# Down products of the six mixers: token block 0 of the first weight piece ahead of the wait for the last outputs

## The chip, the cores and the metric

The kernel runs on one core of one Trainium2 chip, as one program. The metric is the time of one execution on the device, in microseconds (us); lower is better. The time before is the median of three runs.

## What is computed

Two stacks of layers, one behind the other, work on 256 tokens of 1024 values (`x`), all in float32. The first stack has a layer with forgetting attention and one with latent attention, each followed by a mixture of 16 experts. The second has four layers, each a mixer and a squared-ReLU MLP: retention, MoBA attention, differential attention, retention. Each of the six mixers ends with the same step, a product of its outputs with an output matrix (its "down product"), added to `x`:

```python
return o @ w_o                                        # forgetting attention, latent attention
return ((jax.nn.silu(g) * o) @ w_out).astype(h.dtype) # retention: o is 256 x 2048, w_out 2048 x 1024
return (o @ w_out).astype(h.dtype)                    # MoBA, differential attention: o is 256 x 1024
x = x + m
```

In retention `o` has 4 heads of 512 values; in the attentions it has 16 heads of 64 (8 of 128 in the differential one).

## The kernel before

**Engines and order.** Every engine has its instructions written out in program order; semaphores tie them together. There is no scheduler. TensorE does all products and all transposes ("turns"). Float32 precision comes from splitting each operand into a high part and a low part (the rest): a product is high x high, low x high and high x low, three matmuls where one would do.

**The weights.** SyncE streams them in pieces of 128 x 2048 values into a ring `raw` of three. ScalarE copies a piece to its high part (`w_high`, L1813, two instructions), which it may do once `piece_done` says that TensorE is through with the piece three before it. VectorE subtracts to get the low part (`w_low`, L2271). Both rings have three slots, so up to three pieces are ready ahead of TensorE. TensorE waits for `high_ready` (`wait_high`) and `low_ready` (`wait_low`).

**The tokens.** The 256 tokens are two blocks of 128 (`TB` = 2). The sum of a down product, `y_sum`, is the whole PSUM tensor `Y`: token block 0 in its columns 0 to 1023, block 1 in 1024 to 2047.

**A down product** (`down_product`) takes a chunk of 512 rows of the weights as two pieces. Of a piece it does, for both token blocks, 16 matmuls with the high part of the weights (L1169 with the high part of the input, L1171 with the low part), then waits for the low part and does 8 more (L1179): 24 matmuls of 512 columns. The very last piece of a mixer is done block by block (L1159 to L1161), so that VectorE can start to add block 0 to `x`. Attention has 2 such chunks (4 pieces), retention 4 (8 pieces).

**What stands ahead of it in attention.** Eight rounds of heads. Of the last one TensorE weighs the values (`weigh(7)`, L1310) into `o_ps`, which is `Y`'s columns 1024 to 2047. VectorE then splits the turned first half of the outputs (`o_low(0)`, L2334, in the differential layer L2338; it frees the pair buffer of `a.oT[0]`), and after that takes the last round's output out of PSUM (`finish(7)`: L2431, and L2438 or in the differential layer L2440), which raises `o_taken`. TensorE waits for both before the first matmul of the down product. The second half of the outputs is turned between the first piece and the second (`turn_rest`).

**What stands ahead of it in retention.** Head h is weighed into half h % 2 of `Y` (L1601 to L1603). ScalarE squares it (L1826), POOL makes the root mean square (L927, L929), VectorE scales and gates it into `r_o` (`finish(h)`, L2810 and twice L2816), which raises `r_taken`. TensorE turns head h with `turn_round(h)` (8 transposes, L1191) into the pair buffer of `r.oT[h]`; ScalarE and VectorE copy it out in a high part (L1881) and a low part (L2334). Heads 0 and 1 are turned inside the loop, and then come

```python
turn_round(2)
turn_round(3)
for j in range(4):
    wait_emptied(pe, r.oT[j])
    down_product(r.wo[j], *r_blocks(j), j == 0, j == 3)
```

`turn_round(3)` waits for head 3 (half 1 of `Y`), and the first chunk of the down product behind it needs head 0 alone as its input.

Of the kernel before, what the change touches and what calls it, by code (L numbers as in the profile page):

```python
# [14 lines left out]
P = 128  # L15
S = 256
TB = S // P
# [360 lines left out]
def build(nc, w, table, out, rel_scratch):  # L378
# [3 lines left out]
    with ctx:  # L382
# [176 lines left out]
        y_sum = Y[:, :].rearrange("p (b n) -> p b n", b=TB)  # L559
# [15 lines left out]
        piece_done = sem("piece_done")  # L575
# [64 lines left out]
        o_taken = sem("o_taken")  # L640
# [57 lines left out]
        def r_blocks(j):  # L698

            if j < 2:  # L700
                return hT_high[:, 4 * j:4 * j + 4, :], hT_low[:, 4 * j:4 * j + 4, :]
            return gated_high[:, j - 2], gated_low[:, j - 2]
# [270 lines left out]
        def _(pe):  # L973
# [10 lines left out]
            def wait_low(s):  # L984

                pe.wait_ge(low_ready, s + 1)
# [152 lines left out]

                mod_product(m, first_mods[m]).then_inc(modulated, 1)  # L1140

            def down_product(c, high_in, low_in, first, last_one, between=None):

                for j in range(2):
                    if j and between is not None:
                        between()
                    s = 2 * c + j
                    high, low = high_piece(s, 2, D), low_piece(s, 2, D)
                    wait_high(s)
                    if last_one and j == 1:  # L1150

                        wait_low(s)
                        for b in range(TB):
                            bs = slice(b * P, (b + 1) * P)
                            for n in range(2):
                                y, ns = y_sum[:, b, n * 512:(n + 1) * 512], slice(n * 512, (n + 1) * 512)
                                for k in range(2):
                                    hi_in, lo_in = high_in[:, 2 + k, bs], low_in[:, 2 + k, bs]
                                    nc.tensor.matmul(y, hi_in, high[:, k, ns], start=False, stop=False)  # L1159
                                    nc.tensor.matmul(y, lo_in, high[:, k, ns], start=False, stop=False)  # L1160
                                    last = nc.tensor.matmul(y, hi_in, low[:, k, ns], start=False, stop=(k == 1))  # L1161
                            last.then_inc(piece_done if b else first_block_done, 1)
                        continue
                    for b in range(TB):
                        for n in range(2):
                            y, ns = y_sum[:, b, n * 512:(n + 1) * 512], slice(n * 512, (n + 1) * 512)
                            for k in range(2):
                                kk = 2 * j + k
                                nc.tensor.matmul(y, high_in[:, kk, b * P:(b + 1) * P], high[:, k, ns],  # L1169
                                                 start=(first and kk == 0), stop=False)  # L1170
                                nc.tensor.matmul(y, low_in[:, kk, b * P:(b + 1) * P], high[:, k, ns],  # L1171
                                                 start=False, stop=False)
                    wait_low(s)
                    for b in range(TB):
                        for n in range(2):
                            y, ns = y_sum[:, b, n * 512:(n + 1) * 512], slice(n * 512, (n + 1) * 512)
                            for k in range(2):
                                kk = 2 * j + k
                                last = nc.tensor.matmul(y, high_in[:, kk, b * P:(b + 1) * P], low[:, k, ns],  # L1179
                                                        start=False, stop=False)  # L1180
                    last.then_inc(piece_done, 1)
# [75 lines left out]
            def attention(a, dh, q, k, v, qT, kT, o, dv, o_wait, v_wait, gate_at=None, q_wait=None):  # L1257
# [81 lines left out]
                    o_wait(1)  # L1339
                    transposes(a.oT[1], tokpair(o), 4)  # L1340

                pe.wait_ge(o_taken, a.unit + 8)
                for j in range(2):
                    wait_emptied(pe, a.oT[j])
                    down_product(a.wo[j], hT_high[:, 4 * j:4 * j + 4, :], hT_low[:, 4 * j:4 * j + 4, :], j == 0, j == 1,
                                 None if j else turn_rest)

            def attention_done(a):
                def wait(j):
# [223 lines left out]
            def retention(r):  # L1573
# [32 lines left out]
                def turn_round(h):  # L1606
                    pe.wait_ge(r_taken, r.head + h + 1)
                    transposes(r.oT[h], r_o, 4 * h)
# [6 lines left out]
                        turn_round(h - 2)  # L1615
                    weigh(h)
                turn_round(2)
                turn_round(3)
                for j in range(4):
                    wait_emptied(pe, r.oT[j])  # L1620
                    down_product(r.wo[j], *r_blocks(j), j == 0, j == 3)


            pe.wait_ge(rows_loaded, 16 * early)
# [13 lines left out]
            for j in range(6):  # L1638
# [3 lines left out]
                if j == 0:  # L1642
# [5 lines left out]
                                     start=False, stop=True).then_inc(fill_done, 1)  # L1648
                elif j < 5:
                    wait_free(pe, use)  # L1650
                    ps = quads(pair(use)[:, :])
                    for i in range(4):
# [5 lines left out]
                        last = nc.tensor.matmul(ps[:, i, P:S], f1, upto_m, start=False, stop=True)  # L1658
# [21 lines left out]
            for bank in range(4):  # L1680
                for b in range(TB):
                    if b or bank >= 2:
                        turn_latent(b, bank)
                        last = turn_latent(b, bank + 4)
# [37 lines left out]
            for b in range(TB):  # L1722
                for k in range(2):
                    last = nc.tensor.transpose(quads(pair(use)[:, :])[:, k, b * P:(b + 1) * P],
                                               ckv[:, b, k * P:(k + 1) * P], ident)
# [1371 lines left out]
```

## Time and profile before

| | |
|---|---|
| median of 3 runs | 2613.46 us (2613.22 to 2613.64) |
| the profiled execution | 2617.71 us |
| its span, first to last instruction | 2615.9 us |
| TensorE busy | 2463.7 us, 94% of the span, 12650 matmuls |
| VectorE / ScalarE busy | 1699.8 us (65%) / 1318.9 us (50%) |
| mean granted TensorE clock | 0.974 |
| HBM | 533.54 MB read, 206 GB/s over the span |

A busy TensorE is one with a matmul in its pipeline; what it does in a stretch depends also on the clock that it was granted there, full (1.00, 2.4 GHz) or half (0.50, 1.2 GHz). The profiled execution took 4.25 us more than the median of the runs without a profile.

### The profile page before, as it was taken

The numbers are of one execution on the slowest core, as the hardware profiler recorded it, in microseconds if no ns is written. First come the engines' busy times: TensorE is split into PE (matmuls) and PEld (weight loads), VectorE is DVE, ScalarE is ACT, GpSimd is POOL, SyncE is SP. The second block draws the span as 40 slices with busy tenths as digits, with TensorE's granted clock in tenths as the row PEclk, the third lists the DMA queues.
The fourth block names the chain that finished last, engine by engine and source line by source line (L and its number), as shares of the span: only waits on it lengthen the run. The fifth ranks groups of instructions, "written<-read, shape, count | busy, mean of one in ns | idle before, by whom it ended". The sixth has DMA issues, their size and how long they took to land.

```text
span 2615.9 us, 31350 instructions
## 1 busy us (share of the span) xinstructions
PE 2463.7 (94%) x12650; PEld 2082.9 (80%) x12650; DVE 1699.8 (65%) x1521; ACT 1318.9 (50%) x1795; POOL 93.8 (4%) x121
## 2 busy tenths in 40 slices
PE   4989999999989999899999999899997999999999
PEld 3878777787778778779878887688876888987887
DVE  5767888787868776767445555555566655644555
ACT  3555677443646665643444444544445544443543
POOL 1000000101100000000000001000001000000000
PEclk8998999998998999999999999999999999999999
DMA  8714999984716887964535584245551555553553
GB/s 288 276 46 166 319 348 331 364 314 140 285 38 233 312 310 270 337 212 141 195 114 182 177 271 167 91 161 193 193 176 51 185 193 193 177 194 113 177 193 129
DMA packets 229568, 539.80 MB, mean 206 GB/s; under 512 B 20880, under 2 KB 27568, under 8 KB 229424
## 3 DMA queue, kind: packets, MB, share of 16 engines
q1 hardware_dynamic: 207264, 471.82, 51.4%
q0 software_dynamic: 15520, 59.77, 6.4%
q10 hardware_dynamic: 6640, 6.20, 1.2%
q8 instruction: 100, 1.64, 0.2%
q14 instruction: 44, 0.36, 0.0%
HBM read 533.54 MB, written 4.19 MB: 206 GB/s over the span
## 4 chain that ended last, share of the span: by engine, by line
PE 66%; DVE 15%; DMA 8%; ACT 6%; issue 3%; POOL 1%; SPq 1%; ACTq 0%; DVEq 0%; POOLq 0%
PE pair L1032 7%; DVE w_low L2271 6%; PE Y L1169 6%; PE Y L1171 6%; PE Y L1179 6%; PE pair L1073 4%; PE pair L1067 4%; PE pair L1068 4%; PE pair L1040 4%; DMA raw<-in_exp_w_gate 3%; ACT w_high L1813 3%; DMA raw<-in_exp_w_down 3%; PE pair L1002 2%; PE pair L1004 2%; PE pair L1010 2%
## 5 line engine op out<-in xcount | busy, mean ns | idle before, releaser
L2271 DVE TENSOR_TENSOR w_low<-raw,w_high 128x2048 fp32r<-128x2048 f32 (+2 forms) x450 | 1020.7, 2275 | 568.0 <-ACT w_high L1813 565.4
L1813 ACT ACTIVATE w_high<-raw 128x1024 fp32r<-128x1024 f32 (+1 forms) x900 | 910.1, 1050 | 729.9 <-PE Y L1179 202.4
L1067 PE MATMUL pair<-w_high,hT 128*128 128x512 f32 (+1 forms) x596 | 232.4, 391 | 1.3 <-ACT work L1868 0.8
L1068 PE MATMUL pair<-w_high,hT 128*128 128x512 f32 (+1 forms) x596 | 231.0, 388 | 0.0
L1169 PE MATMUL Y<-w_high,gated_high 128*128 128x512 f32 x528 | 205.8, 390 | 0.0
L1171 PE MATMUL Y<-w_high,gated_low 128*128 128x512 f32 x528 | 205.8, 390 | 0.0
L1032 PE MATMUL pair<-hT,w_high 128*128 128x512 f32 x768 | 183.0, 390 | 2.3 <-DVE work L2717 2.3
L1032 PEld LDWEIGHTS pair<-hT,w_high 128*128 128x128 f32 x768 | 142.5, 188 | 31.6 <-DVE work L2717 2.7
L1475 PE MATMUL Y<-w_high,gated_high 128*128 128x512 f32 x320 | 131.4, 411 | 28.0 <-DVE gated_low L2615 23.3
L1431 PE MATMUL pair<-w_high,rounded 128*128 128x512 f32 x384 | 154.1, 401 | 2.7 <-DVE gated_low L2615 2.7
L1432 PE MATMUL pair<-w_high,rounded 128*128 128x512 f32 x384 | 151.6, 395 | 0.0
L1073 PE MATMUL pair<-w_low,hT 128*128 128x512 f32 (+1 forms) x596 | 146.6, 388 | 4.5 <-DVE w_low L2271 4.5
L1073 PEld LDWEIGHTS pair<-w_low,hT 128*128 128x128 f32 x596 | 110.7, 188 | 28.9 <-DVE w_low L2271 6.6
L1067 PEld LDWEIGHTS pair<-w_high,hT 128*128 128x128 f32 x596 | 112.7, 189 | 25.1 <-issue 1.5
L1068 PEld LDWEIGHTS pair<-w_high,hT 128*128 128x128 f32 x596 | 112.7, 189 | 22.4
L1179 PE MATMUL Y<-w_low,gated_high 128*128 128x512 f32 x528 | 130.4, 389 | 0.0
L1477 PE MATMUL Y<-w_high,gated_low 128*128 128x512 f32 x320 | 128.7, 402 | 0.0
L1002 PE MATMUL pair<-hT,w_high 128*128 128x256 f32 x512 | 126.0, 286 | 0.4
L1004 PE MATMUL pair<-hT,w_high 128*128 128x256 f32 x512 | 125.1, 284 | 0.0
L1179 PEld LDWEIGHTS Y<-w_low,gated_high 128*128 128x128 f32 x528 | 99.1, 188 | 20.6
L1169 PEld LDWEIGHTS Y<-w_high,gated_high 128*128 128x128 f32 x528 | 99.2, 188 | 19.9 <-issue 0.2
L1171 PEld LDWEIGHTS Y<-w_high,gated_low 128*128 128x128 f32 x528 | 99.2, 188 | 19.9
(391 smaller groups left out, 4052.7 us busy)
## 6 DMA issues: line engine op xcount, KB each, us to landing
raw<-in_exp_w_gate SPq DMA_DIRECT2D x128, 512.0 KB, 4.5
raw<-in_exp_w_up SPq DMA_DIRECT2D x128, 512.0 KB, 4.8
raw<-in_exp_w_down SPq DMA_DIRECT2D x128, 512.0 KB, 4.6
raw<-in_w_up SPq DMA_DIRECT2D x128, 512.0 KB, 4.7
raw<-in_w_down SPq DMA_DIRECT2D x128, 512.0 KB, 4.4
raw<-in_ret_w_in SPq DMA_DIRECT2D x96, 512.0 KB, 4.7
work<-in_w_mod POOLq DMA_DIRECT2D x40, 1024.0 KB, 7.8
raw<-in_ret_w_out SPq DMA_DIRECT2D x32, 512.0 KB, 4.1
```

What stands on the lines that cost most here:

```text
L1002: nc.tensor.matmul(ps[:, f, :], high[:, k, f * P:(f + 1) * P], hT_high[:, kk, :], start=(kk == 0 and f % 2 == 0), stop=False)
L1004: nc.tensor.matmul(ps[:, f, :], high[:, k, f * P:(f + 1) * P], hT_low[:, kk, :], start=False, stop=False)
L1032: nc.tensor.matmul(ps[:, f, :], high[:, k, fs], hT[:, :, kk, :], start=(kk == 0), stop=False)
L1067: nc.tensor.matmul(ps[:, b, 0:n], in_high[:, k0 + kk, bs], high[:, k, :], start=(kk == 0), stop=False)
L1068: nc.tensor.matmul(ps[:, b, 0:n], in_low[:, k0 + kk, bs], high[:, k, :], start=False, stop=False)
L1073: last = nc.tensor.matmul(ps[:, b, 0:n], in_high[:, k0 + kk, b * P:(b + 1) * P], low[:, k, :], start=False, stop=(kk == k_blocks - 1))
L1169: nc.tensor.matmul(y, high_in[:, kk, b * P:(b + 1) * P], high[:, k, ns], start=(first and kk == 0), stop=False)
L1171: nc.tensor.matmul(y, low_in[:, kk, b * P:(b + 1) * P], high[:, k, ns], start=False, stop=False)
L1179: last = nc.tensor.matmul(y, high_in[:, kk, b * P:(b + 1) * P], low[:, k, ns], start=False, stop=False)
L1431: nc.tensor.matmul(out(m, v), x_high, high[:, k, :], start=(h == 0 and k == 0), stop=False)
L1813: nc.scalar.activation(w_high[:, s % HIGH, part], raw[:, s % RAW, part], ACT.Copy).then_inc(high_ready, 1)
L2271: V.tensor_tensor(w_low[:, s % HIGH, 0:n], part, w_high[:, s % HIGH, 0:n].bitcast(F32), ALU.subtract).then_inc(low_ready, 1)
```

## The change

For the first piece of each mixer's down product, `down_product` gets a function `second_block`. Then the piece is done token block by token block: 8 matmuls with the high weights and 4 with the low ones for block 0, then the call of `second_block`, then the same 12 for block 1. In attention `second_block` is the wait for `o_taken`, which stood ahead of the whole product; in retention it is `turn_round(3)`, with its wait for `r_taken`. Nothing else is changed, on no other engine.

```diff
+                    if j == 0 and second_block is not None:
+
+                        for b in range(TB):
+                            bs = slice(b * P, (b + 1) * P)
+                            if b:
+                                second_block()
+                            for part in (high_in, low_in):
+                                for n in range(2):
+                                    y, ns = y_sum[:, b, n * 512:(n + 1) * 512], slice(n * 512, (n + 1) * 512)
+                                    for k in range(2):
+                                        nc.tensor.matmul(y, part[:, k, bs], high[:, k, ns],
+                                                         start=(first and part is high_in and k == 0), stop=False)
+                            if b == 0:
+                                wait_low(s)
+                            for n in range(2):
+                                y, ns = y_sum[:, b, n * 512:(n + 1) * 512], slice(n * 512, (n + 1) * 512)
+                                for k in range(2):
+                                    last = nc.tensor.matmul(y, high_in[:, k, bs], low[:, k, ns], start=False, stop=False)
+                        last.then_inc(piece_done, 1)
                         continue
...
-                pe.wait_ge(o_taken, a.unit + 8)
+                def outputs_taken():
+                    pe.wait_ge(o_taken, a.unit + 8)
+
...
-                                 None if j else turn_rest)
+                                 None if j else turn_rest, None if j else outputs_taken)
...
-                turn_round(3)
+
+                def turn_last():
+                    turn_round(3)
+
                 for j in range(4):
                     wait_emptied(pe, r.oT[j])
-                    down_product(r.wo[j], *r_blocks(j), j == 0, j == 3)
+                    down_product(r.wo[j], *r_blocks(j), j == 0, j == 3, second_block=None if j else turn_last)
```

TensorE's order in the first retention, from the last matmul of head 3 on; before, with both turns ahead of the product:

```order
L1603 MATMUL Y<-work 128x512
L1191 MATMUL pair<-squares,work 128x128 [waits emptied1,r_taken]
L1191 MATMUL pair<-squares,work 128x128 x7
L1191 MATMUL pair<-squares,work 128x128 [waits emptied0,r_taken]
L1191 MATMUL pair<-squares,work 128x128 x7
L1169 MATMUL Y<-w_high,hT 128x512 [waits high_ready,emptied1]
L1171 MATMUL Y<-w_high,hT 128x512
...
L1179 MATMUL Y<-w_low,hT 128x512 [waits low_ready]
L1179 MATMUL Y<-w_low,hT 128x512 x7
```

The same place in the changed kernel (the turns are L1211 there, the matmuls of the first piece L1174 and L1181):

```order
L1625 MATMUL Y<-work 128x512
L1211 MATMUL pair<-squares,work 128x128 [waits emptied1,r_taken]
L1211 MATMUL pair<-squares,work 128x128 x7
L1174 MATMUL Y<-w_high,hT 128x512 [waits high_ready,emptied1]
L1174 MATMUL Y<-w_high,hT 128x512 x7
L1181 MATMUL Y<-w_low,hT 128x512 [waits low_ready]
L1181 MATMUL Y<-w_low,hT 128x512 x3
L1211 MATMUL pair<-squares,work 128x128 [waits emptied0,r_taken]
L1211 MATMUL pair<-squares,work 128x128 x7
L1174 MATMUL Y<-w_high,hT 128x512 x8
L1181 MATMUL Y<-w_low,hT 128x512 x4
```

Twelve of the 24 matmuls of the first piece now stand between the turn of head 2 and the turn of head 3.

TensorE's order in the differential attention, from the last weighing on; before:

```order
L1310 MATMUL Y<-work 128x128 [waits o_taken,pT_ready]
L1310 MATMUL Y<-work 128x128 x7
L1169 MATMUL Y<-w_high,hT 128x512 [waits high_ready,emptied0,o_taken]
L1171 MATMUL Y<-w_high,hT 128x512
...
L1179 MATMUL Y<-w_low,hT 128x512 [waits low_ready]
L1179 MATMUL Y<-w_low,hT 128x512 x7
L1191 MATMUL pair<-squares,work 128x128 [waits emptied1,o_ready]
```

And in the changed kernel:

```order
L1330 MATMUL Y<-work 128x128 [waits o_taken,pT_ready]
L1330 MATMUL Y<-work 128x128 x7
L1174 MATMUL Y<-w_high,hT 128x512 [waits high_ready,emptied0]
L1174 MATMUL Y<-w_high,hT 128x512 x7
L1181 MATMUL Y<-w_low,hT 128x512 [waits low_ready]
L1181 MATMUL Y<-w_low,hT 128x512 x3
L1174 MATMUL Y<-w_high,hT 128x512 [waits o_taken]
L1174 MATMUL Y<-w_high,hT 128x512 x7
L1181 MATMUL Y<-w_low,hT 128x512 x4
L1211 MATMUL pair<-squares,work 128x128 [waits emptied1,o_ready]
```

The wait for `o_taken` has moved behind the first 12 matmuls; the wait for the freed pair buffer (`emptied`) stays ahead of them.

## Rows read from the trace of the kernel before

**Rows 1.** The page, part 1: span, and busy time of each engine.
```profile
span 2615.9 us, 31350 instructions
PE 2463.7 (94%) x12650; PEld 2082.9 (80%) x12650; DVE 1699.8 (65%) x1521; ACT 1318.9 (50%) x1795; POOL 93.8 (4%) x121
```

**Rows 2.** Waits of PE: waiter <- releaser: us in total, times, longest us.
```profile
PE Y L1310 <- ACT work L1934: 26.4, 28, 2.7
...
PE pair L1191 <- DVE work L2816: 6.3, 4, 2.8
...
PE Y L1169 <- DVE work L2438: 2.2, 3, 0.7
...
PE Y L1169 <- DVE work L2440: 2.1, 1, 2.1
```

**Rows 3.** Timeline of PE, first retention (start, duration, instruction, idle before).
```profile
1349.05 1.09 PE L1191 MATMUL pair<-squares,work 128*128 128x128 f32 x8 [0.38 <-DVE work L2816]
1352.91 1.97 PE L1191 MATMUL pair<-squares,work 128*128 128x128 f32 x8 [2.77 <-DVE work L2816]
1354.53 0.77 PE L1169 MATMUL Y<-w_high,hT 128*128 128x512 f32 x1
1355.11 0.63 PE L1171 MATMUL Y<-w_high,hT 128*128 128x512 f32 x1
...
1358.91 0.39 PE L1169 MATMUL Y<-w_high,hT 128*128 128x512 f32 x1
1359.14 0.40 PE L1171 MATMUL Y<-w_high,hT 128*128 128x512 f32 x1
...
1362.11 0.39 PE L1169 MATMUL Y<-w_high,hT 128*128 128x512 f32 x1
```

**Rows 4.** Timeline of DVE and of ACT, first retention.
```profile
1334.29 2.28 DVE L2271 TENSOR_TENSOR w_low<-raw,w_high 128x2048 fp32r<-128x2048 f32 x1
...
1348.91 1.22 DVE L2334 TENSOR_TENSOR hT<-pair,hT 128x1024 fp32r<-128x1024 f32 x1
...
1351.45 1.41 DVE L2816 SCALAR_TENSOR_TENSOR work<-Y,head_rs,work 128x512 f32<-128x512 f32 x2
...
1355.97 1.23 DVE L2334 TENSOR_TENSOR gated_low<-pair,gated_high 128x1024 fp32r<-128x1024 f32 x1 [1.98 <-ACT gated_high L1881]
1364.35 2.29 DVE L2271 TENSOR_TENSOR w_low<-raw,w_high 128x2048 fp32r<-128x2048 f32 x1 [7.15 <-ACT w_high L1813]
...
1362.31 2.01 ACT L1813 ACTIVATE w_high<-raw 128x1024 fp32r<-128x1024 f32 x2 [6.37 <-PE Y L1179]
```

**Rows 5.** Windows around the first turn 3: engines, then PEclk, DMA share, GB/s.
```profile
1349.05:1352.02 2.97, 1.09 (x8) 0.85 (x8) 1.81 (x3) 2.14 (x5) 0.89 (x2) 1.00 0.00 0
1352.02:1358.85 6.83, 5.94 (x18) 5.06 (x19) 3.19 (x4) 1.02 (x1) 0.00 (x0) 0.50 0.00 0
```

**Rows 6.** Timeline of PE, second retention.
```profile
2384.15 1.97 PE L1191 MATMUL pair<-squares,work 128*128 128x128 f32 x8 [2.77 <-DVE work L2816]
...
2393.15 0.39 PE L1169 MATMUL Y<-w_high,hT 128*128 128x512 f32 x1
```

**Rows 7.** Timelines of DVE and PE: forgetting, MoBA (1697), differential attention (2018 on).
```profile
177.52 1.22 DVE L2334 TENSOR_TENSOR hT<-pair,hT 128x1024 fp32r<-128x1024 f32 x1 [1.64 <-ACT hT L1902]
...
179.35 0.50 PE L1169 MATMUL Y<-w_high,hT 128*128 128x512 f32 x1 [0.73 <-DVE work L2438]
...
1697.60 0.79 PE L1169 MATMUL Y<-w_high,hT 128*128 128x512 f32 x1 [0.73 <-DVE work L2438]
...
2018.20 1.66 DVE L2338 SCALAR_TENSOR_TENSOR hT<-pair,subln,hT 128x256 fp32r<-128x256 f32 x4 [3.03 <-ACT hT L1904]
...
2020.73 0.56 PE L1169 MATMUL Y<-w_high,hT 128*128 128x512 f32 x1 [2.10 <-DVE work L2440]
2026.08 1.98 PE L1179 MATMUL Y<-w_low,hT 128*128 128x512 f32 x8
```

**Rows 8.** Window from the first retention's product to MoBA: PE busy, PEclk, DMA.
```profile
1362.00:1651.00 289.00, 284.59 (x1442) 1.00 0.60 194
```

More of the change, by code:

```diff
@@ L1140, in first_modulation, with down_product @@
                 mod_product(m, first_mods[m]).then_inc(modulated, 1)
-            def down_product(c, high_in, low_in, first, last_one, between=None):
+            def down_product(c, high_in, low_in, first, last_one, between=None, second_block=None):
                 for j in range(2):
@@ L1162, in down_product @@
                             last.then_inc(piece_done if b else first_block_done, 1)
+                        continue
+                    if j == 0 and second_block is not None:
[16 more added lines that the diff above has]
+                        last.then_inc(piece_done, 1)
                         continue
```

## The prediction, made before the changed kernel ran

> **What bounds the kernel now.** I read the page first. TensorE has a matmul in flight for 2463.7 of 2615.9 us, and no other engine comes near [rows 1]. So time is gained where TensorE has nothing to do, or where it works at half clock. Next, its list of waits, for those that stand beside the lines of the diff [rows 2]. The reader should see how small they are. The wait of a down product for the last output (L1169 on L2438) is 2.2 us over three attentions, 0.73 each, and on L2440 2.1 us in the differential one. The transposes L1191 wait 6.3 us in four places for L2816; two of these places are the turn of head 3, 2.77 us each [rows 3, 6]. That is 2.2 + 2.1 + 5.5 = 9.8 us of idle time that the change can touch.
>
> Then the timeline of the first retention, for what such a gap costs beside itself [rows 3]. Turn 2 takes 1.09 us for 8 transposes, turn 3, behind the gap, 1.97 us. The matmuls behind it start 0.42 to 0.43 us apart (1355.11 is followed by one at 1355.53; the shown pair at 1358.91 and 1359.14 is 0.23 apart). The windows say why [rows 5]: the granted clock is 1.00 until 1352.02, in the middle of the gap, and 0.50 from there to 1358.85. The level fell from 2.4 to 1.2 GHz after TensorE had stood still. So the gap costs twice.
>
> Last, who could take the gain away. From the end of the first piece to MoBA's rounds TensorE is busy for 284.59 of 289 us at full clock [rows 8]. Weights come in time there: after a piece ends, ScalarE needs 2.01 us and VectorE 2.29 us to make the next one, and both idle before it (6.37 and 7.15 us) [rows 4]. What starts earlier therefore ends earlier.
>
> **Retention, first.** Turn 2 starts at 1349.05. Its 8 transposes take some 0.9 us to the start of what follows (the slow set: 1.97 us busy, but 1.62 to the next matmul; in proportion 1.09 gives 0.9) [rows 3]. Block 0's 12 matmuls can start at 1349.95:
> - Their input, head 0, was freed by the same semaphore (`emptied1`) for which turn 2 waits.
> - Half 0 of `Y`, where they write, held head 2, which `r_taken` of turn 2 covers.
> - The low weights of the first piece are no later than 1336.57, the end of the last subtraction before this place (1334.29 + 2.28) [rows 4].
>
> 12 x 0.23 = 2.8 us, with some 0.08 for the switch: they end at 1352.8. VectorE is done with head 3 at 1351.45 + 1.41 = 1352.86 [rows 4], and turn 3 starts at 1352.91 as now. The other buffer that it needs is freed at 1348.91 + 1.22 = 1350.13. So turn 3 moves by nothing: the gap is filled by half a piece. After it come 0.9 us of turn, now at full clock, and 2.8 us of block 1: the second piece starts at 1352.91 + 3.7 = 1356.6, where it starts at 1362.11 now. **Gain 5.5 us**: 2.77 of idle, and 2.7 of clock (turn 0.7, ten matmuls at 0.2).
>
> **Retention, second.** The same with 2384.15 and 2393.15 [rows 6]: 2387.85 for 2393.15, **gain 5.3 us**.
>
> If only the idle time comes back and the clock is as slow as now, each is worth 2.77, half of it.
>
> **Attention.** The first matmul still waits for the buffer that `o_low(0)` frees; VectorE does `finish(7)` behind it. In the first attention o_low ends at 177.52 + 1.22 = 178.74, and a released matmul starts some 0.06 later: 178.80 for 179.35 [rows 7]. Gain 0.55. The wait is as long in three places (2.2 us in 3) [rows 2], so **1.65 us** for three. In the differential one o_low ends at 2018.20 + 1.66 = 2019.86, so 2019.9 for 2020.73 [rows 7]: **0.8 us**. Block 1 comes 2.8 us after block 0, when `o_taken` is long raised. In MoBA the first matmul is slow already (0.79 us, 0.50 in the first attention) [rows 7]; 0.55 us earlier at half speed is worth 0.3 if the clock rises no sooner. In the differential one the first 16 matmuls take 2026.08 - 2020.73 = 5.35 us, where 16 x 0.23 = 3.7: the clock costs 1.6 us there. A gap of 1.3 instead of 2.1 us may or may not spare it; I don't count it, and keep it for the range.
>
> **Nothing is added.** The piece has 24 matmuls as before, each with its own weight load. `high x high` and `low x high` come in another order, with the same operand sizes. The turns of head 3 go behind half a piece, and their copies (ScalarE, then VectorE to 1355.97 + 1.23 now [rows 4]) are needed by the fourth chunk, six pieces of 24 x 0.23 = 5.5 us later. SyncE and POOL have nothing moved.
>
> **Sum.** 5.5 + 5.3 + 1.65 + 0.8 = 13.3 us off the profiled execution's 2617.7, so 2604.4 for it. Its own time lies 4.25 above the median; I take the same gain off the median: 2613.46 - 13.3 = **2600.2 us**.
>
> **The ends.** Low gain: idle alone, 2 x 2.77 + 1.1 + 0.3 + 0.8 = 7.7, 2605.7 us. High gain: the differential clock (1.6) and in MoBA the 14 slow matmuls (2.8) as well: 17.7, 2595.8 us.
>
> **A rule to weigh.** In rows 3 and 5 the slow time behind the gap is 6.83 us, in one execution. The Trainium skill, TensorE: Matmul & The Clock Gate, section What's actually happening, says that the clock gate's default is the throttled state, that activity releases it, and that the number of slow matmuls changes from run to run of the same kernel (6, 11 or 14). By it, the 2 x 2.7 us of clock are no fixed price: the sum would be anywhere between the two ends above, where by the row it is 13.3. One execution's trace can't tell whether the number changes here; that the clock fell while TensorE stood still agrees with it.
>
> **Rivals.**
> - *The clock gives back nothing.* It falls behind turn 3 or elsewhere near by all the same, or the timed runs before did not have the fall that the profile shows. For it: the profile is 4.25 us slower than the median. Against: both retentions show the fall, at the same gap. 2605.7 us. Chance 0.18.
> - *Given back downstream.* Where the shift meets a stage that waits for something not moved (a DMA, POOL), it ends. Were both retention gains lost, 1.65 + 0.8 would stay: 2611.0 us. Against it: rows 8, and everything behind a mixer starts from its sum. 0.04.
> - *It doesn't do what it says*, since block 0 is held by the buffer or by the low weights. The timeline leaves no room for it in retention; 2612 to 2613 us. 0.02.
> - *Slower.* The shifts move the later stages against the granted clock, and new slow stretches appear in the waits of the attention rounds (28 waits on L1934, 26.4 us in all [rows 2]). One such stretch costs what MoBA's does, 14 x 0.2 = 2.8 us. Five eat up the gain, and from seven on the kernel is slower by over 0.2%: 2613.46 - 13.3 + 7 x 2.8 = 2619.8 us. 0.01.
>
> **How the numbers follow.** My forecast has 0.75. One or two slow stretches more or fewer lie within it (2.8 us each way). A measurement here tells 0.2%, 5.2 us, from no change; every case but the last three ends below 2608.2. Faster 0.93, same 0.06, slower 0.01. The range takes in both ends: 2595.8 to 2605.9.
>
> **What would show it.** In the changed kernel's profile: 12 matmuls (L1174, L1181) between the turns L1211 of heads 2 and 3; turn 3 idle by under 0.3 us where it is 2.77, and 1.1 us long instead of 1.97; a granted clock of 1.00 through both places; the second piece 3.7 us after the start of turn 3. In the attentions, an idle time of 0.2 us ahead of L1174 where it is 0.73, and some 1.3 where it is 2.10, now put down to L2359 or L2363, the splits. **What would make me wrong:** block 0 at half clock (12 x 0.43 = 5.1 us, turn 3 then 2.2 us later), a later stage whose idle time grows by what was gained, or slow stretches at other places than now.

## The result, and the profile after

The changed kernel took 2593.04 us (median of 13 runs, 2585.54 to 2607.46), the kernel before 2613.22 us (13 runs, 2596.83 to 2621.91). The ratio is 0.9933, 95% interval 0.9918 to 0.9949: 13 to 21 us faster. I had forecast 2600.2 us, 13.3 us faster, with a range from 2595.8 to 2605.9. The direction was right, the time lies 2.8 us below the range. The two medians stand 20.2 us apart, the means of the same 13 runs each 2610.2 and 2594.2, 16.0 us apart.

The profiled execution of the changed kernel took 2607.46 us, by chance the slowest of its 13. Its page:

```profile
span 2605.7 us, 31350 instructions
...
PE 2456.4 (94%) x12650; PEld 2076.5 (80%) x12650; DVE 1700.1 (65%) x1521; ACT 1317.9 (51%) x1795; POOL 93.5 (4%) x121
```

The waits of PE in the changed kernel, the rows that answer to [rows 2] (L1330 is the old L1310, L1211 the old L1191, L2841 the old L2816, L1174 the first matmuls of a first piece):

```profile
PE Y L1330 <- ACT work L1959: 26.4, 28, 2.7
...
PE Y L1174 <- DVE hT L2363: 1.3, 1, 1.3
PE pair L1211 <- DVE work L2841: 0.8, 2, 0.4
```

The wait of the transposes (L1211) for the gated heads (L2841) fell from 6.3 to 0.8 us. The two places of 2.77 us are gone; what stays are two of 0.38. No wait for the last output stands ahead of a down product any more; in the differential attention 1.29 us are left, for the split of the first half (L2363).

The timeline of PE in the first retention, to set beside [rows 3], with VectorE's rows:

```profile
1351.10 1.09 PE L1211 MATMUL pair<-squares,work 128*128 128x128 f32 x8 [0.38 <-DVE work L2841]
1351.95 2.07 PE L1174 MATMUL Y<-w_high,hT 128*128 128x512 f32 x8
1353.86 1.07 PE L1181 MATMUL Y<-w_low,hT 128*128 128x512 f32 x4
1354.95 1.09 PE L1211 MATMUL pair<-squares,work 128*128 128x128 f32 x8
1355.80 2.07 PE L1174 MATMUL Y<-w_high,hT 128*128 128x512 f32 x8
1357.71 1.07 PE L1181 MATMUL Y<-w_low,hT 128*128 128x512 f32 x4
1358.62 0.39 PE L1189 MATMUL Y<-w_high,hT 128*128 128x512 f32 x1
...
1353.49 1.41 DVE L2841 SCALAR_TENSOR_TENSOR work<-Y,head_rs,work 128x512 f32<-128x512 f32 x2
```

Block 0's 12 matmuls fill the gap almost to the end. Turn 3 starts 3.85 us after turn 2, where it was 3.86: VectorE's 1353.49 + 1.41 = 1354.90 still sets it. From turn 2 to the second piece it is 7.52 us, where [rows 3] have 1362.11 - 1349.05 = 13.06. That is 5.54 us; I had written 5.5. The window, to set beside [rows 5], shows the clock at 1.00 throughout (the last but two of its numbers):

```profile
1351.10:1358.62 7.52, 7.49 (x41) 6.19 (x41) 5.00 (x6) 3.16 (x6) 0.88 (x2) 1.00 0.00 0
```

And the differential attention, the answer to the last of [rows 7]:

```profile
2014.01 2.05 PE L1330 MATMUL Y<-work 128*128 128x128 f32 x16 [1.11 <-ACT work L1959]
2017.36 2.11 PE L1174 MATMUL Y<-w_high,hT 128*128 128x512 f32 x8 [1.29 <-DVE hT L2363]
2019.30 1.07 PE L1181 MATMUL Y<-w_low,hT 128*128 128x512 f32 x4
2020.21 1.98 PE L1174 MATMUL Y<-w_high,hT 128*128 128x512 f32 x8
...
2023.73 0.47 PE L1189 MATMUL Y<-w_high,hT 128*128 128x512 f32 x1
```

The 8 matmuls from 2017.36 take 2.11 us, not the 3.4 of half clock. From the last weighing to the second piece it is 9.72 us, where the first trace of before has 12.12.

### The profile page after: what moved, and what is told of

It reads as the page before. It is cut to its first block, busy times and chain, and to the rows that moved or that the text cites. A ratio compares the mean times of both kernels' runs of the same rounds, so it can differ in the third digit from the quotient of the medians.

```text
span 2605.7 us, 31350 instructions
## 1 busy us (share of the span) xinstructions
PE 2456.4 (94%) x12650; PEld 2076.5 (80%) x12650; DVE 1700.1 (65%) x1521; ACT 1317.9 (51%) x1795; POOL 93.5 (4%) x121
## 4 chain that ended last, share of the span: by engine, by line
PE 65%; DVE 15%; DMA 8%; ACT 6%; issue 3%; POOL 1%; SPq 1%; ACTq 0%; DVEq 0%
DVE w_low L2296 6%; PE pair L1032 6%; PE Y L1189 5%; PE Y L1191 5%; PE Y L1199 5%; PE pair L1073 4%; PE pair L1067 4%; PE pair L1068 4%; ACT w_high L1838 3%; PE pair L1040 3%; DMA raw<-in_exp_w_down 3%; DMA raw<-in_exp_w_gate 3%; PE pair L1002 2%; PE pair L1004 2%; PE pair L1010 2%
## 5 line engine op out<-in xcount | busy, mean ns | idle before, releaser
L1191 PE MATMUL Y<-w_high,gated_low 128*128 128x512 f32 x528 | 205.8, 390 | 0.0
L1191 PEld LDWEIGHTS Y<-w_high,gated_low 128*128 128x128 f32 x528 | 99.2, 188 | 19.9
```

## The experiments

Theory A was my prediction's: the gain is what the six places show, and what lies beyond it is scatter of single runs. Theory A2 is the same with the places' means over several traces instead of one trace. Rivals: B, a further gain somewhere else; C, the fall of the clock at the gap is luck of one execution; D, the order of the operands is itself worth something.

Two measures are used. **Times** are means with 1.96 standard errors; for the kernel before all its 153 runs together (those of `aa_before` and `aa_before2` among them), mean 2610.0 us, standard deviation 6.5, so most single runs lie within some 25 us. **Places** are read from the timelines: from the start of turn 2 (retention), or of the last 16 weighing matmuls (attention), to the first matmul of the second piece. In attention the turn of the second half lies inside the place. (Expectations that were written earlier count from anchors slightly ahead: 3.1 us more in retention, 0.3 in the MoBA and differential attentions.) All traces, in us:

```
kernel         forgetting  latent  retention 1  MoBA  differential  retention 2
before               9.09    9.12        13.05  11.92        12.12        12.86
aa_before           11.91   11.87        10.27  10.48        12.18        11.62
aa_before2          10.58    9.14        11.58  11.89        12.12        10.27
order_only           9.10    9.12        10.28  11.91        12.10        10.27
lite_before          9.11    9.10        10.24  11.92        12.14        12.85
busy_gap             9.09   11.91        12.62  11.90        10.52        12.65
busy_gap12          11.91    9.10        10.27  11.95        12.14        10.24
att_fill             9.10    9.10        11.89  10.43        10.52        11.89
ret_only             9.10   11.87         7.55  11.88        12.14         7.53
ret_only2           10.63   11.87         7.53  11.88        10.53         7.55
att_only            10.05    8.58        11.67  10.15         9.73        11.86
att_only2            8.54    8.54        12.89  10.13         9.74        11.67
after                9.92    9.92         7.52   9.97         9.72         7.55
aa_after             8.54    9.97         7.55  10.12         9.71         7.56
aa_after2            8.55    8.55         7.56   9.87         9.72         7.55
lite_after           9.91    8.55         7.56  10.07         9.71         7.53
high_first           9.74    9.80         7.56   8.16         9.59         7.56
```

**The same kernels again** (no edit).

> The kernel before once more, unchanged. Theory A (the change is worth its local gains, 13 us or so, and the rest of the 20.2 us between the two medians is scatter of single runs): ratio 1.000 within 0.3%, and single runs scattered over some 20 us as in the first 13. Both retentions show the idle 2.77 us ahead of the turn of head 3 and a granted clock that falls at it, in this second trace as in the first. Rival B (a systematic further gain of 4 to 7 us): says the same of this run. Rival C (the fall of the clock at the gap was luck of one execution): one or both retentions keep the clock at 1.00 here, and the second piece starts 2.7 us sooner than in the first trace.

> The changed kernel once more, unchanged. Theory A: 12 to 17 us below before, ratio 0.9935 to 0.9955; turn of head 3 without idle time and clock at 1.00 in both retentions; in the trace the two retentions gain 5.5 and 5.3 us again against the kernel before, and only the attentions and the expert stages differ from the first trace. Rival B: 17 to 20 us below again, ratio 0.9925 to 0.9935.

Measured: `aa_before` ratio 1.001 (0.9988 to 1.0031), `aa_after` 0.9932 (0.9908 to 0.9956). The ratio of `aa_after` lies just in rival B's range; its mean, 2594.3 us, is 15.0 us below that of the 35 runs of the kernel before beside it, in theory A's. It doesn't tell the two apart. The scatter is as expected. The retentions' gain of 5.5 and 5.3 us did not come again: it is 2.7 and 4.1 between these two traces. Rival C was right in one of two places: in the first retention of `aa_before` the gap is there and the clock doesn't fall.

```profile
1344.74 1.09 PE L1191 MATMUL pair<-squares,work 128*128 128x128 f32 x8 [0.38 <-DVE work L2816]
1348.60 1.09 PE L1191 MATMUL pair<-squares,work 128*128 128x128 f32 x8 [2.77 <-DVE work L2816]
1349.44 0.47 PE L1169 MATMUL Y<-w_high,hT 128*128 128x512 f32 x1
...
1355.01 0.39 PE L1169 MATMUL Y<-w_high,hT 128*128 128x512 f32 x1
```

Behind the same 2.77 us, turn 3 takes 1.09 us and the second piece starts 10.27 us after turn 2, where the first trace had 13.05. So the clock's part of the gap is 0 to 2.8 us from one execution to the next, while the idle part is 10.27 - 7.55 = 2.7 in each.

> The kernel before a third time, for the mean of its runs and one more trace. Mean 2610 within 3 us; retentions 13.4 to 16.2 us from the anchor to the second piece, differential attention 12.4 to 12.5, first two attentions 9.1 or 11.8, MoBA 10.8 or 12.2.

> The changed kernel a third time. Mean 2594 within 3 us; retentions 10.65 us in both, differential 10.03, the other attentions 8.5 to 10.5. Theory A2: the means of the kernels stand 13 to 16 us apart over all runs.

Measured: 12 runs each, medians 2610.33 and 2595.60, ratio of the second to before 0.9953 (0.9934 to 0.9971). The places of the changed kernel are as expected; of `aa_before2` the second retention is at 10.27 from turn 2, without a fall, and the forgetting attention at 10.58, between the two values that I had named. Over all runs: before 2610.0 (153 runs), changed 2594.3 (37 runs, median 2593.9): **15.6 us, plus or minus 2.6**.

**The halves.** `ret_only` puts the attentions' wait back ahead of the piece, `att_only` the turn of head 3:

```diff
-                def outputs_taken():
-                    pe.wait_ge(o_taken, a.unit + 8)
+                pe.wait_ge(o_taken, a.unit + 8)
...
-                                 None if j else turn_rest, None if j else outputs_taken)
+                                 None if j else turn_rest)
```

```diff
-                def turn_last():
-                    turn_round(3)
+                turn_round(3)
...
-                    down_product(r.wo[j], *r_blocks(j), j == 0, j == 3, second_block=None if j else turn_last)
+                    down_product(r.wo[j], *r_blocks(j), j == 0, j == 3)
```

> Only the retentions are changed; in attention the wait for the last output stands ahead of the whole first piece as before (the piece is still done block by block? no: in the old order). Theory A: the two local gains alone, 10.8 us, ratio 0.996; ahead of the first down matmul of the three attentions 0.73 us idle as before. Rival B, if the further gain came from the retentions: 15 us or more.

> Only the attentions are changed; the retentions turn head 3 ahead of the product as before. Theory A: 0.55 us at three places and 0.8 at the differential one, 2.5 us, and up to 2.8 us more or less at each for the clock: 2 to 6 us, ratio 0.998 to 0.999. Rival B, if the further gain came from the attentions: 7 to 10 us, ratio 0.9965. Retentions as before, with 2.77 us idle and the clock at 0.50 behind it.

> Only the retentions changed, a second time, for the mean. By the places in the traces it is worth 7.7 us (3.6 and 4.1); the first 12 runs stand 10.7 us below the mean of before, with an uncertainty of some 3. Theory A2: together nearer to 8 to 9; nearer to 11 would say that something outside the two places gains too.

> Only the attentions changed, a second time. By the places it is worth 5.5 us, of which 1.2 are given back between MoBA and the differential attention; the first 12 runs stand 7.0 below the mean of before. Theory A2: together 4.5 to 6; the differential attention's place 10.0 us again.

Measured: the retentions alone 0.9961 (0.9943 to 0.9979) and 0.997 (0.9947 to 0.9992), together 24 runs, mean 2601.7, 8.2 us plus or minus 2.7 below before. The attentions alone 0.9974 (0.995 to 0.9998) and 0.9976 (0.9955 to 0.9998), together 24 runs, mean 2604.1, 5.9 plus or minus 2.2. The first 12 runs of `att_only` (7.3 plus or minus 2.8 us below before, ratio 0.9974) missed theory A's 2 to 6 us and lie on rival B's side; the second 12 gave 4.5. Of `ret_only` the first 12 gave 11.0 and the second 5.4. Together both halves end where A2 expects them. The sum, 14.1, is the whole change's 15.6 within its uncertainty. The waits of PE in `att_only` show what a moved wait leaves:

```profile
PE pair L1211 <- DVE work L2838: 6.3, 4, 2.8
...
PE Y L1174 <- DVE hT L2360: 1.3, 1, 1.3
...
PE Y L1174 <- DVE hT L2356: 0.5, 3, 0.2
```

0.73 us became 0.2 in three attentions and 2.10 became 1.29, as forecast; the retentions' 6.3 us stand as they were. Their places take 11.67 to 12.89 us, so the clock behind the gap was low for a shorter time there than in the first trace of the kernel before.

**Order alone.** The calls do nothing, the waits and turn 3 stand ahead:

```diff
-                def outputs_taken():
-                    pe.wait_ge(o_taken, a.unit + 8)
+                pe.wait_ge(o_taken, a.unit + 8)
+
+                def outputs_taken():
+                    pass
...
+                turn_round(3)

                 def turn_last():
-                    turn_round(3)
+                    pass
```

> The first piece is done block by block, as in the changed kernel, but the waits and the turn of head 3 stand ahead of the whole piece, as before. Theory A2: no gain from the order of the matmuls, ratio 1.000 within 0.3%; 2.77 us idle ahead of the turn of head 3, and 0.7 and 2.1 us ahead of the attentions' pieces. A rival D, that the other order of operands in a piece is itself worth something: 2 us or more faster, and block 0 and 1 of a piece shorter than 5.45 us together at full clock.

Measured: 1.0012 (0.9995 to 1.0028), 12 runs. The waits are those of the kernel before (2.77 us, 0.7 and 2.1). Rival D falls: the timeline has the same 2.77 us and then a piece of the same length in the new order. It starts at 1342.26 and the next one at 1347.83, 5.57 us, as in `aa_before` from 1349.44 to 1355.01.

```profile
1341.41 1.09 PE L1211 MATMUL pair<-squares,work 128*128 128x128 f32 x8 [2.77 <-DVE work L2844]
1342.26 2.09 PE L1174 MATMUL Y<-w_high,hT 128*128 128x512 f32 x8
1344.19 1.08 PE L1181 MATMUL Y<-w_low,hT 128*128 128x512 f32 x4
1345.11 1.98 PE L1174 MATMUL Y<-w_high,hT 128*128 128x512 f32 x8
```

**Filling the gap with needless work** (the kernel before, and in the second run 12 for 24):

```diff
                 turn_round(2)
+                keep_busy(24)
                 turn_round(3)
```

> The kernel before, with 24 needless matmuls of 128 columns between the turns of head 2 and head 3, into a free part of Y: TensorE does not stand still, but nothing useful is done. It splits the retention's gain in clock and idle time. Theory A2: turn 3 starts when it did, at full clock always; from turn 2's predecessor to the second piece 13.4 us in both retentions, where the traces before had 13.4 to 16.2 and the changed kernel 10.7: 1.6 us each on average, ratio 0.9985 within 0.3%. Had the clock nothing to do with the gap, the place would take 13.4 to 16.2 as before.

> As busy_gap, with 12 needless matmuls for 24, since 24 took 5.4 us and held the turn of head 3 back by 2.4 us. 12 take 2.7 us and fit the gap. Theory A2 (the clock falls because TensorE stands still there): turn 3 starts 3.86 us after turn 2, as before, and the clock stays at 1.00 in both retentions; 13.4 us in both places, where five traces of the old turn order have 13.4 to 16.2, mean 14.2 and 15.0. Against before that is 2.4 us for both, ratio 0.999, hardly to be told. If the clock falls at either place all the same, the gap isn't its cause.

Measured: `busy_gap` 1.0004 (0.9988 to 1.0021). Its filler was too long, since 24 calls are 48 matmuls in the trace: turn 3 starts 2.4 us late, and the places take 12.62 and 12.65 us. The clock stayed at 1.00 over both:

```profile
1333.82 1.09 PE L1191 MATMUL pair<-squares,work 128*128 128x128 f32 x8 [0.38 <-DVE work L2817]
1334.75 5.52 PE L1198 MATMUL Y<-squares 128*128 128x128 f32 x48
1340.11 1.04 PE L1191 MATMUL pair<-squares,work 128*128 128x128 f32 x8
```

```profile
1333.82:1346.44 12.62, 12.62 (x89) 11.67 (x89) 5.00 (x6) 3.16 (x6) 0.89 (x2) 1.00 0.01 1
```

`busy_gap12` fits: 0.9998 (0.998 to 1.0016), and in its timeline

```profile
1338.63 1.09 PE L1191 MATMUL pair<-squares,work 128*128 128x128 f32 x8 [0.38 <-DVE work L2817]
1339.56 2.84 PE L1198 MATMUL Y<-squares 128*128 128x128 f32 x24
1342.48 1.09 PE L1191 MATMUL pair<-squares,work 128*128 128x128 f32 x8
```

turn 3 starts 3.85 us after turn 2, and both places take 10.27 and 10.24 us, with the clock at 1.00 over each. That agrees with A2: no fall in four places (two traces) with the gap filled by needless work. Unfilled gaps had no fall in 5 of 16 places either, so four places alone would prove little. What carries more weight is that with the gap filled by real work, 14 of 14 places (seven traces) took 7.52 to 7.56 us.

**The differential attention.** Needless matmuls ahead of the attentions' wait, in the kernel before:

```diff
+                keep_busy(9 if a is plan.diff.att else 3)
                 pe.wait_ge(o_taken, a.unit + 8)
```

> The kernel before, with needless matmuls of 128 columns into a free part of Y ahead of the attentions' wait for the last output: 9 in the differential attention, where TensorE stands still for 2.10 us, 3 in the others, where it is 0.73. It tells what of the attentions' gain is clock. Theory A2 (the differential attention's clock falls because of the 2.10 us): its place takes 10.8 to 10.9 us at full clock, 1.6 below the 12.42 to 12.50 of six traces of the old order, though the piece starts no sooner; then 1.6 of its 2.4 us gain in the changed kernel is clock. If it still takes 12.4, the fall comes from the rounds ahead, and the changed kernel's gain needs another cause. The other three: as before, 9.1 or 11.8 and 10.8 or 12.2.

Measured: the place takes 10.52 us where the first trace has 12.12, with the piece starting no sooner, as theory A2 expects. But the trace shows more, one round of heads ahead of the place:

```profile
1990.73 2.08 PE L1310 MATMUL Y<-work 128*128 128x128 f32 x8 [2.73 <-ACT work L1935]
1992.59 1.78 PE L1191 MATMUL pair<-squares,work 128*128 128x128 f32 x8
...
1996.36 2.05 PE L1310 MATMUL Y<-work 128*128 128x128 f32 x16 [1.11 <-ACT work L1935]
1998.24 2.17 PE L1198 MATMUL Y<-squares 128*128 128x128 f32 x18
...
2004.27 1.98 PE L1179 MATMUL Y<-w_low,hT 128*128 128x512 f32 x8
```

The same eight weighing matmuls in the first trace of the kernel before:

```profile
2012.55 1.16 PE L1310 MATMUL Y<-work 128*128 128x128 f32 x8 [2.73 <-ACT work L1934]
```

They take 2.08 us for 1.16, and the turn behind them 1.78 us: the clock had already fallen there, before the filler came. Two other traces of the old order, `busy_gap` and `ret_only2`, have 10.52 and 10.53 us at the place without a filler, and in both the clock fell in that same round. So the three traces without a fall at the place had it one round earlier, and this experiment doesn't show what the filler did. It doesn't show either that 1.6 us of the gain are clock, since a fall that moves ahead is paid for there. To see that, the place has to be taken together with the stretch from MoBA's second piece to the differential attention's last weighing:

| | traces | stretch ahead | place | together |
|---|---|---|---|---|
| wait of 2.10 us, fall at the place | 7 | 309.6 to 310.7 | 12.10 to 12.18 | 321.8 to 322.9 |
| wait of 2.10 us, fall in the round ahead | 2 | 310.9 and 311.2 | 10.52 and 10.53 | 321.5 and 321.7 |
| the same, with the filler (`att_fill`) | 1 | 311.3 | 10.52 | 321.8 |
| wait of 1.29 us | 6 | 310.6 to 313.6 | 9.71 to 9.74 | 320.3 to 323.3 |

In each of the six traces with the 1.29 us wait the clock falls in the stretch ahead, some 6 or some 40 us before the place; with the 2.10 us wait it does so in four of ten. The change gains 2.1 us at the place, but 0.6 plus or minus 1.0 us over the two together (means of nine traces and six, `att_fill` left out). That is the 0.8 us of idle time, with no gain in clock to be seen.

The time of `att_fill`, 0.9963 (0.9939 to 0.9987), 10 runs, mean 8.2 plus or minus 4.5 us below before, is more than the places explain; this I can't account for but by scatter.

**Without the experts' share of the weight stream.** The kernel before and the changed one, each leaving out half of the bytes of every expert piece, so that the experts' outputs are other ones:

```diff
+                    if expert:
+                        if kk == 4:
+                            quarters = [(dst[:, 0:1], part[:, 0:1]), (dst[:, 2:3], part[:, 2:3])]
+                        else:
+                            quarters = [(dst[:, 0:1, 0:512], part[:, 0:1, 0:512]), (dst[:, 1:2, 0:512], part[:, 1:2, 0:512])]
```

> The kernel before, but of each piece of expert weights only half the bytes are loaded; the other half keeps what was in the ring, so the experts' outputs are wrong. It is one half of a pair with the next kernel. The two expert stages took from 411 to 427 us in the six traces so far; if their scatter is one of the weight stream, they are shorter and steadier here. No forecast against the kernel before but that it is faster, by 10 to 60 us.

> The changed kernel with the same halved loads of the experts. Against the one before it in this call. Theory A2 (all of the gain lies at the six places: retentions 4.3 us each on average, the first three attentions 0.5 to 1.5, the differential one 2.4, sum 14.5): 12.5 to 16.5 us between the two medians. Rival B (part of the gain is made in the expert stages, from where the traces differ by up to 10 us): under 12 us here, with the expert stages as long in both.

Measured: medians 2581.44 and 2570.77 us. The first is some 28 us below the kernel before, as expected. The medians stand 10.7 us apart, below what A2 expected and on rival B's side; the means, 6 runs each, 12.0 plus or minus 5.6. That can't tell 12 from 15. The two traces put 11.5 us behind turn 2 of the first retention (1266.2 us to the end, and 1254.7). Between the first two attentions, where the first expert stage lies, the changed kernel took 3.1 us longer (543.8 and 546.9). Inconclusive.

**A further step.** In the changed kernel the wait for the pair buffer is split, high part first:

```diff
                             for part in (high_in, low_in):
+                                if b == 0 and part is low_in and lows is not None:
+                                    lows()
...
-                    wait_emptied(pe, a.oT[j])
+                    if j:
+                        wait_emptied(pe, a.oT[j])
+                    else:
+                        pe.wait_ge(hT_high_made, a.high + 1)
```

> The changed kernel, with the first piece's wait for the freed pair buffer split: the four matmuls with the high part of the outputs wait for ScalarE's high part alone, and the wait for VectorE's low part stands ahead of the four with the low part. Theory A2 (what is left idle ahead of the piece is the split): in the differential attention the first matmul starts right after the last weighing, where it stands idle 1.29 us in the changed kernel, and the place is 0.9 us shorter, 9.1 for 10.03; 0.2 us in the three others; 1.5 us in all against the changed kernel, ratio to before 0.9925 to 0.994. No gain, if the high part is late too.

Measured: 0.9944 (0.9925 to 0.9964), 6 runs, mean 1.6 plus or minus 6.2 us above the changed kernel's. The ratio is just outside the expected 0.9925 to 0.994, and 1.5 us more or less can't be told from six runs. In the trace the first matmul starts right behind the weighing, as expected, but the place takes 9.59 us for 9.72, and not 0.9 us less:

```profile
2014.13 2.05 PE L1332 MATMUL Y<-work 128*128 128x128 f32 x16 [1.11 <-ACT work L1965]
2015.94 1.17 PE L1176 MATMUL Y<-w_high,hT 128*128 128x512 f32 x4
2017.47 1.21 PE L1176 MATMUL Y<-w_high,hT 128*128 128x512 f32 x4 [0.36 <-DVE hT L2369]
...
2022.88 1.09 PE L1213 MATMUL pair<-squares,work 128*128 128x128 f32 x8 [0.53 <-DVE work L2448]
...
2021.59 1.23 DVE L2448 TENSOR_TENSOR work<-work,rs 128x1024 f32<-128x1024 f32 x1 [2.85 <-POOL rs L929]
```

A new wait takes the gain: behind the first piece TensorE turns the second half of the outputs, which VectorE scales (L2448) only when POOL's root mean square (L929) is there. In the changed kernel that wait was already close:

```profile
2021.47 1.23 DVE L2442 TENSOR_TENSOR work<-work,rs 128x1024 f32<-128x1024 f32 x1 [2.84 <-POOL rs L929]
2022.94 1.03 PE L1211 MATMUL pair<-squares,work 128*128 128x128 f32 x8
```

VectorE was done at 2022.70 and TensorE came at 2022.94, so no more than 0.2 us could be had. The differential attention is now bound by that chain.

## Why the prediction was wrong, and where it was right

**What failed is the step "I take the same gain off the median: 2613.46 - 13.3", and the range built on it.** I took three runs within 0.4 us of each other for the kernel's time. The 153 runs average 2610.0 us with a standard deviation of 6.5: the three stood 3.5 us high, and nothing on record makes their closeness more than chance. My range had terms for the clock at the six places and none for the runs' own scatter. From 2610.0 the same sum gives 2596.7 us, inside the range; the changed kernel's mean over 37 runs is 2594.3. So of the 7.2 us between forecast and median, 3.5 are the base, 2.3 the size of the gain (15.6 for 13.3, less than its uncertainty), and 1.3 that the median of the 13 runs lies below the mean of all. That the profile was slower than the median, which I noted, says nothing in this light.

**The sum of 13.3 was near in size, but its terms were not: the retentions' were too large and most of the attentions' too small, and that they cancel is luck.** The whole change measures 15.6 plus or minus 2.6 us. By the places, as means of the old order (8 or 9 traces) less means of the new one (7 or 6), it is 13.9:

| place | forecast | measured by places |
|---|---|---|
| retention 1 and 2 | 5.5 and 5.3 | 3.9 and 4.1 |
| forgetting, latent | 0.55 each | 0.8 and 1.3 |
| MoBA | 0.55 | 1.7 |
| differential | 0.8 | 2.1 |
| sum | 13.3 | 13.9 |

Against the 13.9 stand 1.4 plus or minus 1.0 us by which the stretch between MoBA and the differential attention is longer in the new order, which leaves 12.5. The clock falls there in all six traces of the new order and in three of the nine of the old; why it does so more often is not shown.

- *Retention, mechanism.* Right, to a tenth of a us: 5.54 between the two first traces, turn 3 not moved, block 0 within the gap. The size was wrong: I put the clock's part at 2.7 us as if it were fixed. It is 0 to 2.8, on average 3.9 - 2.7 = 1.2 and 4.1 - 2.7 = 1.4. The rule that I weighed is that the number of slow matmuls changes from run to run (the Trainium skill, TensorE: Matmul & The Clock Gate, What's actually happening). The page tells it of a kernel's start; the traces show the same behind a gap: 10.27, 11.58 and 13.05 us at one place of one program (`aa_before`, `aa_before2`, `before`). I should have let it move the sum, not only the range.
- *Attention.* The idle time was right (0.73 to 0.2, 2.10 to 1.29). Of the differential attention's 1.6 us of clock I wrote "I don't count it". At the place that looks like a miss: six of six places with the 1.29 us wait kept full speed, seven of nine with 2.10 did not. Over the place and the stretch ahead the gain is 0.6 plus or minus 1.0 us, so the 0.8 that I counted stands, and a gain in clock is not shown. In MoBA the shorter wait was worth more than itself, 1.7 plus or minus 0.3 us for 0.55. In the first two attentions together it was 2.1 plus or minus 1.5 for 1.1, which may be no more than the idle time.
- *Nothing is added*: right, `order_only` shows no change.
- *Who could take the gain away*: right for the last layers. In all 17 traces it is 351.6 us from the differential attention's second piece to turn 2 of the second retention, and 222.8 from the second retention's second piece to the end, to within 0.05. So what is gained at these two places stands to the end. It is less simple behind the first retention. If the two first traces are laid beside each other matmul by matmul, 1.6 of its 5.5 us are lost in the MLP, where TensorE waits 2.3 us for L2742 (L2717 before) in both, and the clock falls at that wait in the changed kernel's trace only. It falls there in 13 of the 17 traces, of both orders, so the change is not its cause. The whole stretch to MoBA takes 331.8 to 335.1 us, on average 333.8 in the old order and 334.0 in the new.
- *Rivals.* "The clock gives back nothing" did not come about as a whole, but in half of the retentions' clock part. Slow stretches at new places, which *Slower* named, did appear ahead of the differential attention, at a cost of 1.4 us, a tenth of the gain. The two others did not show.

**What stays open.** From turn 2 of the first retention to the end, the five traces with the old order of waits and turns throughout and no filler (`before`, `aa_before`, `aa_before2`, `order_only`, `lite_before`) take 1263.9 to 1266.9 us and four of the changed kernel (`lite_after` among them) 1251.5 to 1254.7: 11.4 plus or minus 1.9 us on average, for 12.15 forecast (5.5, 5.3, 0.55 and 0.8). There the account closes. The 4 us that are left of 15.6 would lie ahead of it, where I forecast 1.1 and the two places give 2.1, and where traces of one program differ by 24 us. So whether the expert stages gain something (rival B) is not settled. Nor is the cause of a fall of the clock at a given gap in a given execution. For the 2.77 us gap the runs show only that it was frequent with the gap (11 of 16 places) and absent without (18 of 18, four of them with needless work).

## What to carry to other kernels

When TensorE waits for the last part of a result ahead of an accumulation, do that share of the accumulation first that neither reads nor overwrites it. Here the two token blocks lie in different halves of the PSUM tensor, which makes it possible. Count the gap in matmuls (2.77 us held 12 of 0.23), and look for the next wait behind the one that goes, since in the differential attention it was only 0.2 us away. Here a gap cost its idle time in every trace and a clock term only on average. Take that term from several traces, and with it the stretch ahead, where a fall that goes missing at the place may have happened. Take the base from many runs, not from three that happen to agree.

## What the runs showed of the hardware

- One program's granted clock differs from execution to execution at the same place behind the same wait: from turn 2 to the second piece 10.27 to 13.05 us in three traces of the kernel before, all with the 2.77 us of idle time. Without it, seven traces have 7.52 to 7.56.
- Half clock can be missing at a place and stand just ahead of it instead. Behind the 2.10 us wait of the differential attention, seven traces of nine have it at the place (12.10 to 12.18 us), and the two others in the round of heads ahead (10.52 and 10.53 us).
- A place can be slow with no long wait directly ahead. In MoBA of the changed kernel the first 8 matmuls take 3.53 us, at half clock, with 0.14 us of idle time ahead of them; the longer wait, 1.11 us, stands ahead of the last weighing:

```profile
1693.34 2.03 PE L1330 MATMUL Y<-work 128*128 128x64 f32 x16 [1.11 <-ACT work L1959]
1695.52 3.53 PE L1174 MATMUL Y<-w_high,hT 128*128 128x512 f32 x8
1698.88 1.08 PE L1181 MATMUL Y<-w_low,hT 128*128 128x512 f32 x4
```

- Single runs of one program on one core scatter by 39 us (2592 to 2631). In the traces nearly all of it lies in the first part, with the experts: in three traces of the changed kernel it is 1326.8 to 1351.1 us up to turn 2 of the first retention, and 1251.5 to 1254.6 behind it.
